# Three instead of five updates per step in a block inverse, and its stores and loads moved to later steps

## The reference

```
xn   = rmsnorm(h, norm_w);  proj = xn @ w_in          # 2048 x 14368 columns
u_pool, z_pool, q, k, v, z_dn, b, a, gate_pool, gate_dn = split(proj)
y_pool = causal_multiscale_pool(u_pool) * silu(z_pool)
y_dn   = gated_deltanet_branch(q, k, v, z_dn, b, a)   # 16 heads of 128, chunks of 64
merged = sigmoid(gate_pool) * (y_pool @ w_pool_out) + sigmoid(gate_dn) * (y_dn @ w_dn_out)
out    = rmsnorm(h + merged @ w_o)[16:]
```

```
lmat = where(strict, (k_beta @ k^T) * decay, 0)
tmat = triangular_solve(eye + lmat, eye)              # lower, 9 chunks x 16 heads
u_c, w_c = tmat @ v_beta, tmat @ (k_beta * exp(gcum))
```

## Time and profile before

| | us |
|---|---|
| Median of 3 runs | 2085.02 |
| Lowest and highest run | 2084.86, 2086.17 |
| The profiled execution, its own time | 2085.02 |
| Its span (first to last instruction of the record) | 2083.4 |
| TensorE busy | 2010.5 |
| VectorE busy | 940.1 |
| ScalarE busy | 778.6 |
| Mean granted clock of TensorE | 0.985 |

### The profile page before, as it was taken

How to read it: one execution, slowest core, us unless ns; L and a number is a source line. 1 busy time by engine, 2 the same in 40 slices (tenths; PEclk the granted TensorE clock), 3 DMA queues, 4 the chain that set the end, 5 groups by cost and what they waited for, 6 DMA issues and landing times.

```text
span 2083.4 us, 35885 instructions
## 1 busy us (share of the span) xinstructions
PE 2010.5 (96%) x13284; PEld 1727.7 (83%) x13284; DVE 940.1 (45%) x2487; ACT 778.6 (37%) x2236; POOL 96.8 (5%) x125
## 2 busy tenths in 40 slices
PE   6999999999999999999999999999999999999996
PEld 5888898888888888887889877788888888888885
DVE  6333344645555464554645544422223544434332
ACT  6322224335353443534335353432233422224333
POOL 4000000000000000000000000000000000000000
PEclk9999999999999999999999999999999999999998
DMA  6133322223132231232323223334336344345221
GB/s 225 46 108 117 119 90 87 74 76 109 42 106 78 76 103 62 86 95 78 83 65 89 89 85 96 96 118 140 105 112 230 126 142 127 115 142 211 83 79 81
DMA packets 233834, 218.33 MB, mean 105 GB/s; under 512 B 63177, under 2 KB 219682, under 8 KB 233026
## 3 DMA queue, kind: packets, MB, share of 16 engines
q1 hardware_dynamic: 167090, 180.23, 26.3%
q10 hardware_dynamic: 60960, 17.24, 3.4%
q0 software_dynamic: 5632, 18.79, 2.7%
HBM read 193.80 MB, written 23.05 MB: 104 GB/s over the span
## 4 chain that ended last, share of the span: by engine, by line
PE 89%; DMA 4%; DVE 3%; issue 1%; ACT 1%; ACTq 1%; POOL 0%; DVEq 0%; SPq 0%
PE pj L512 78%; PE pg L512 7%; PE pt L512 2%; DMA st<-inverse_scratch 2%; DMA inverse_scratch<-oo 1%; DVE oo L1387 1%; DVE oo L1390 1%; PE pt L647 1%; DMA oo<-gram_scratch 1%; ACTq L970 0%; PE pg L791 0%; ACTq L971 0%; DVE wl L1170 0%; POOL xl L1650 0%; DVE fst L1195 0%
## 5 line engine op out<-in xcount | busy, mean ns | idle before, releaser
L512 PE MATMUL pj<-xh,wh 128*128 128x264 f32 (+2 forms) x2688 | 752.8, 334 | 4.6 <-DVE wl L1170 3.3
L512 PE MATMUL pj<-xh,wl 128*128 128x264 f32 (+2 forms) x2688 | 719.6, 322 | 4.3 <-issue 4.3
L512 PE MATMUL pj<-xl,wh 128*128 128x264 f32 (+2 forms) x2688 | 721.2, 323 | 0.0
L1170 DVE TENSOR_TENSOR wl<-raw,wh 128x256 fp32r<-128x256 f32 x896 | 356.8, 430 | 601.2 <-ACT wh L832 601.1
L512 PEld LDWEIGHTS pj<-xh,wh 128*128 128x128 f32 x2688 | 449.1, 190 | 68.7 <-issue 26.4
L512 PEld LDWEIGHTS pj<-xh,wl 128*128 128x128 f32 x2688 | 449.9, 190 | 43.5 <-issue 4.9
L512 PEld LDWEIGHTS pj<-xl,wh 128*128 128x128 f32 x2688 | 449.6, 190 | 35.2 <-issue 1.0
L832 ACT ACTIVATE wh<-raw 128x256 fp32r<-128x256 f32 x896 | 313.1, 407 | 129.6 <-issue 75.9
L832 ACT ACTIVATE wh<-rawb 128x256 fp32r<-128x256 f32 x288 | 97.9, 406 | 182.5 <-PE pj L512 181.5
L512 PE MATMUL pj<-yh,wh 128*128 128x512 f32 x384 | 149.4, 389 | 0.0
L512 PE MATMUL pj<-yl,wh 128*128 128x512 f32 x384 | 149.4, 389 | 0.0
(11 more groups left out here) (201 smaller groups left out, 1641.5 us busy)
## 6 DMA issues: line engine op xcount, KB each, us to landing
raw<-in_w_in SPq DMA_DIRECT2D x112, 1024.0 KB, 5.1
rawb<-in_w_dn_out SPq DMA_DIRECT2D x16, 1024.0 KB, 6.0
rawb<-in_w_o SPq DMA_DIRECT2D x12, 1024.0 KB, 5.5
gates_scratch<-stg ACTq DMA_DIRECT2D x32, 256.0 KB, 2.0
rawb<-in_w_pool_out SPq DMA_DIRECT2D x8, 1024.0 KB, 5.5
gst<-gates_scratch POOLq DMA_DIRECT2D x32, 256.0 KB, 3.0
yraw<-branch_scratch SPq DMA_DIRECT2D x1, 5632.0 KB, 22.0
xt<-in_x SPq DMA_DIRECT2D x4, 1024.0 KB, 6.2
```

The lines of the kernel that those rows point to most:

```text
L512: return pe.matmul(dst, lhs, rhs, start=start, stop=stop)
L1170: tt(wl[:, j, 2 * q:2 * q + 2, :], raw[:, 2 * par + h, 2 * q:2 * q + 2, c * P:(c + 1) * P], wh[:, j, 2 * q:2 * q + 2, :].bitcast(F32), ALU ...
```

## The change

It alters three numbers. `NSTEP` goes from 5 to 3: the 14 updates of the substitution take steps 15 to 19 instead of 15 to 17 (5, 5, 4 before; 3, 3, 3, 3, 2 now), and the copy stands in step 19. ScalarE issues the stores of the inverted blocks in step 20 instead of 18, and the loads in step 22 instead of 21. TensorE's wait for the loads stays in step 24. No semaphore is added and no instruction's work is altered.

```
@@ -377,7 +377,7 @@
         F0 = G0 + GC
         V0 = F0 + 7
         W0 = F0 + 9
-        NSTEP = 5
+        NSTEP = 3
         L0 = W0 + 9
@@ -960,11 +960,11 @@
-                if m == W0 + 3:
+                if m == W0 + 5:
                     wait(w_turned, 1, 1)
                     for scratch, block_of in zip(inv_d, (wblk, wtr)):
...
-                if m == W0 + 6:
+                if m == W0 + 7:
                     wait(w_stored, 32, 32)
                     for h in range(2):
```

## The result

The kernel became slower, by more than twice as much as predicted: 2116.5 us (median of 4 runs, 2116.2 to 2117.9) against 2085.6 us (the three runs of before and a fourth). The ratio is 1.0149, with a 95% interval of 1.0132 to 1.0167. The prediction was 2098.9 us, with a range up to 2111.

The account below looks back on a forecast made before the run. The prediction took TensorE as the bound, busy 2010.5 of 2083.4 us, with its eight `st` waits lengthened. It summed 2085.0 + 13.9 (cut substitution) + 0 (`raw` meeting stores and loads) + 0 (clock) = 2098.9 us, range 2090 to 2111.

Parts of the forecast that it names:

- The chain without slack: Substitution, stores, loads, TensorE run serially in each pair; any lengthening is paid eight times, `st` waits rising 30.5 to about 44 us.
- The cut substitution: VectorE's splits and convolution taps fall between the updates: 1.92 us more in seven pairs, 0.42 in the eighth, 13.9 us.
- `raw` moves ahead of the stores: SyncE issues the next 1 MB weight piece near 630.8, one microsecond ahead of the stores instead of after them.
- The stores may lose 0 to 1.8 us and the loads gain 0 to 1.8: Per pair, stores now meet `raw` and loads run alone; +14.4 to -14.4 us over eight pairs, taken as 0.
- The Trainium skill's rule: HBM latency 0.2 us on average, 2 us at high load: stores' round trip grows an estimated 1.8 us a pair, loads' shrinks likewise.
- the first rival: Stores suffer from `raw` and loads gain nothing: 14.4 us more, 2113.3 us if fully paid; 12% chance.
- ScalarE's queue and the held stand: ScalarE's wait for the copy moves from step 18 to 20; work queued behind stores and loads costs nothing, freeing it gains nothing.
- The inserted splits: VectorE's splits now between the updates find ScalarE's `wh` pieces ready, so waiting for inputs costs nothing more.
- The clock: TensorE's lower-clock stretch after each wait may change by at most 1.4 us a pair; taken as 0, +-6 us.
- The third, the clock: Longer idle lengthens TensorE's lower-clock stretch in about half the pairs: 5.6 us more, 2104.5 us; 13% chance.
- The not-slower one: Loads land alone in 2.5 instead of 4.3 us, stores lose nothing: 14.4 us given back, 2084.5 us; 5% chance.
- The fourth: ScalarE's stand at step 18 had a hidden cost that its shift to a shorter stand gives back; 2093 us, 2% chance.

Follow-up runs that it names:

- Experiment 5: Kernel before with four updates per step instead of five, stores and loads in their old steps; ratio 1.0036 to the kernel before.
- experiment 2: Changed kernel with SyncE holding `raw` until the loads have landed; ratio 1.0021 to the kernel before.
- experiment 1: Changed kernel with SyncE holding `raw` until the stores have landed; ratio 1.0137 to the kernel before.
- experiment 7: Kernel before with all 14 updates in one step, stores in step 16, loads in step 20, `raw` not held; ratio 1.0039 to the kernel before.
- experiment 8: Changed kernel with the `raw` piece that meets the stores moving half its bytes, except in the eighth pair; 2101.2 us in one execution.
- experiment 9: Changed kernel with the `raw` piece that meets the stores moving a quarter of its bytes, except in the eighth pair; 2101.7 us in one execution.
- Experiment 3: Kernel before, still five updates per step, with only stores moved to step 20 and loads to step 22; ratio 1.0004 to the kernel before.
- experiment 4: Kernel before with `raw` held until the loads have landed; 2073.3 us against 2090.0, ratio 0.9921.
- experiment 6: Kernel before with all 14 updates in one step, stores in step 16, loads in step 20, `raw` held until loads land; 2058.5 us, ratio 0.9859.

## Why the prediction was wrong

**The chain without slack: right.** The waits account for 30.4 of 30.9 us, though they rose to 60.9 us and not to about 44.

**The cut substitution: right, 1.7 us too small.** 13.9 us were predicted, 15.6 measured (2.16 instead of 1.92 us in seven pairs, 0.45 instead of 0.42 in the eighth). The difference is the 0.35 us of standing ahead of the first tap, less 0.06 us for each of the two later taps. What VectorE stands for there isn't settled: the profile names nothing, and no experiment was aimed at it. Experiment 5 shows the same arithmetic with one tap.

**`raw` moves ahead of the stores: right,** at 1.0 us ahead, as worked out.

**The stores may lose 0 to 1.8 us and the loads gain 0 to 1.8, "I take half of each, and they cancel: 0": the step that failed.** The stores lost 2.8 to 3.2 us a pair, 23.8 in sum, and the loads gained 1.1, 8.8 in sum: +15.0 us where 0 stood. With this term the sum of the prediction would have been 2114. The bound was wrong because it took the 4.3 us of the kernel before for the price of a transfer that meets `raw`. Those loads came 1.4 to 3.45 us behind `raw`, and the last of them, for which TensorE waits, met only its tail. The other end was wrong too: 2.5 us is a write, and the loads alone take 3.1 us (experiment 2), so they had little more than the 1.1 us to gain that they gained. Experiments 1 and 7 give the whole price of a meeting, 2.7 to 2.9 us (6.01 and 5.78 against 3.10), and experiments 8 and 9, with the packets of the two queues, show that it is time spent behind `raw`'s bytes. Taking the midpoint of two bounds that belonged to different overlaps made the error look balanced. That the two sides would be unequal could have been seen: the loads' rows showed a meeting that was half over, the timeline put the stores into the middle of one.

**The Trainium skill's rule** that I weighed ("DMA: Bandwidth & Descriptors", "Latency and other measured facts": 0.2 us of HBM latency on average, 2 us at high load) gave the right direction for the stores and, with 2113 us in the first rival, a figure near the time. The runs say that it was not the cause: the stores' packets had not begun to move, and once they did they took 1.8 us in place of 1.7 (third pair). The same page has another rule, in "Queues, rings and completion order": each DMA engine takes turns between the queue rows that have work, a whole packet at a time. The trace after doesn't agree with it: from 643 to 646 us `raw` moved 848 packets and the stores none. The eighth pair of experiment 3, where the stores came first, does: 846 packets of stores beside 783 of `raw` in 3 us. Why turns are dealt in one case and not in the other stays open.

**ScalarE's queue and the held stand: right.** Experiment 3 puts the moved steps at +0.04% (-0.05 to +0.14%). The inserted splits found their inputs ready, too: VectorE stands ahead of none of them in the third pair.

**The clock: right in sum, by luck in each pair.** The stretches at the lower clock add to 36.6 us after and 36.5 before. The longer standing did not change them. Experiments 4 and 6 show that they can change: 27.3 us with waits near 2.6 us, 13.7 us with waits of 1.6 to 2.3.

**The rivals.** The first one, the stores' side, is what happened, less the loads' gain; it had 12% and its 2113 us lay outside the stated range. The third, the clock, gave nothing: the stretches at the lower clock have the same sum. The not-slower one needed the opposite sign of the same term and is refuted. The fourth (a gain from freeing ScalarE) is refuted by experiment 3.

## What to carry to other kernels

A transfer on the critical path must be looked at together with what else is issued within some microseconds of it, also from other queues and for other purposes: here a prefetch whose buffer was free in step 19 and whose weights are first split about 20 steps later decided 15 of 31 us, because a change of VectorE's order moved its issue by 3 us. Do not price such a meeting from a transfer that meets only part of it; first line up the issue times. And where a prefetch has slack, hold it behind the landing of the transfer that has none: that one wait took 0.8% off the kernel before, and with a compact substitution 1.4%.

## What was not expected of the hardware

A 1 MB transfer of long rows, issued on another queue 1 us ahead of two 72 KB stores of short rows, made them 2.9 us later, while it landed itself in 5.3 us (the median of all such transfers after, 5.1 before): the cost falls on the small transfers alone. They hardly shared the engines with it: none of their packets moved for 3.3 to 3.5 us, in any of the eight pairs. Issued 0.3 to 0.6 us behind the loads, it made the last of them 2.7 to 2.9 us later.

The lower clock after a wait was in every pair with waits of 2.5 us or more, and absent in four of the eight pairs of experiment 6, with waits of 1.6 to 2.3 us: of the waits of 1.68, 1.55, 1.86 and 1.62 us none was followed by it, and those of 1.71 and 1.82 us were. So whether it comes can't be told from the wait's length alone.
